# Keys' high rope rows, low rope rows and high nope rows in one 128-row tile; low nope keys as one 64-row product per head

## The reference, cut to what matters

```python
q = (rmsnorm(cq, q_norm_g) @ w_uq).reshape(bsz, S, B_HEADS, B_NOPE + B_ROPE)   # 16 heads, 64 + 32
qn, qr = q[..., :B_NOPE], apply_rope(q[..., B_NOPE:], cos, sin)
...
s = (jnp.einsum('bqhd,bkhd->bhqk', qn_b, kn_all)            # 768 keys: 256 of the context, 512 tokens
     + jnp.einsum('bqhr,bkr->bhqk', qr_b, kr_all)).astype(jnp.float32) * scale
p = jax.nn.softmax(s, axis=-1).astype(dt)
return jnp.einsum('bhqk,bkhd->bqhd', p, v_all)
```

## Time and profile before

| what | value |
|---|---|
| median of 3 runs | 1159.51 us (1159.49 to 1160.32) |
| the profiled execution | 1159.5 us |
| its span on the core | 1157.7 us |
| granted TensorE clock, mean | 0.997 of full speed |
| PE busy | 1099.8 us, 95% of the span |
| DVE busy | 734.3 us, 63% |
| ACT busy | 649.0 us, 56% |
| POOL busy | 419.3 us, 36% |
| layer B's attention | from 562.8 us to some 735 us of the span |

### The profile page before, as it was taken

How to read it: one execution, slowest core, us unless ns; L and a number is a source line. 1 busy time by engine, 2 the same in 40 slices (tenths; PEclk the granted TensorE clock), 3 DMA queues, 4 the chain that set the end, 5 groups by cost and what they waited for, 6 DMA issues and landing times.

```text
span 1157.7 us, 20235 instructions
## 1 busy us (share of the span) xinstructions
PE 1099.8 (95%) x7430; PEld 900.7 (78%) x7430; DVE 734.3 (63%) x1590; ACT 649.0 (56%) x1355; POOL 419.3 (36%) x513
## 2 busy tenths in 40 slices
PE   5999999999998899999899999999999999999996
PEld 2678778877885689877688887898878777888785
DVE  7575766676568625363787787745767775527745
ACT  5604555555556526643677777846567753457733
POOL 2633012212120334675400002416654326456781
PEclk9999999999999999999999999999999999999998
DMA  9741424322114521130201101053212403213112
GB/s 373 253 163 46 176 107 162 133 108 101 46 29 173 204 81 37 40 109 35 57 14 34 65 10 47 1 166 87 73 46 78 151 19 128 91 56 121 44 37 73
DMA packets 34253, 109.33 MB, mean 94 GB/s; under 512 B 4516, under 2 KB 7076, under 8 KB 33772
## 3 DMA queue, kind: packets, MB, share of 16 engines
q1 hardware_dynamic: 34156, 108.05, 27.7%
HBM read 101.39 MB, written 2.11 MB: 89 GB/s over the span
## 4 chain that ended last, share of the span: by engine, by line
PE 75%; DVE 12%; ACT 5%; issue 3%; POOL 2%; DMA 2%; SPq 1%; DVEq 0%; POOLq 0%; ACTq 0%
PE PS L677 31%; PE PS L660 15%; PE PS L794 8%; PE PS L782 7%; PE PS L983 6%; PE PS L1051 3%; DMA AF<-wstream 2%; PE PS L712 2%; DVE AD L2372 1%; ACT AF L1272 1%; DVE AF L2069 1%; POOL AR L2553 1%; DVE AR L2273 1%; PE PS L884 1%; PE PS L693 1%
## 5 line engine op out<-in xcount | busy, mean ns | idle before, releaser
L2553 POOL TENSOR_TENSOR AR<-AF,AR 128x256 fp32r<-128x256 f32 x396 | 304.5, 802 | 585.2 <-ACT AR L1152 585.2
L677 PE MATMUL PS<-AR 128*128 128x512 f32 (+1 forms) x2208 | 450.5, 360 | 4.7 <-POOL AR L2553 1.4
L677 PEld LDWEIGHTS PS<-AR 128*128 128x128 f32 x2208 | 364.0, 189 | 72.6 <-issue 10.5
L660 PE MATMUL PS<-AR 128*128 128x256 f32 (+4 forms) x1284 | 244.9, 327 | 6.7 <-ACT AF L1272 1.7
L660 PEld LDWEIGHTS PS<-AR 128*128 128x128 f32 (+1 forms) x1284 | 179.8, 190 | 41.7 <-issue 20.6
L1281 ACT ACTIVATE AF<-PS 128x512 f32<-128x512 f32 (+3 forms) x192 | 124.6, 649 | 100.0 <-PE PS L782 96.0
L1272 ACT ACTIVATE AF<-PS,AF 128x512 f32<-128x512 f32 (+3 forms) x192 | 140.8, 733 | 27.2 <-DVE AF L2349 18.3
L782 PE MATMUL PS<-AF 128*128 128x128 f32 x864 | 127.4, 274 | 8.4 <-DVE AF L1990 5.9
L782 PEld LDWEIGHTS PS<-AF 128*128 128x128 f32 x864 | 100.1, 140 | 32.9 <-issue 15.5
L1152 ACT ACTIVATE AR<-AF 128x1024 fp32r<-128x1024 f32 x99 | 103.3, 1052 | 35.3 <-PE PS L983 27.9
L794 PE MATMUL PS<-AF 128*64 128x128 f32 x1728 | 115.3, 278 | 3.4 <-DVE AF L1997 2.5
(11 more groups left out here) (216 smaller groups left out, 1147.2 us busy)
## 6 DMA issues: line engine op xcount, KB each, us to landing
AF<-wstream SPq DMA_DIRECT2D x171, 512.0 KB, 5.0
AF<-x_in SPq DMA_DIRECT2D x2, 1024.0 KB, 8.5
AD<-rows SPq DMA_DIRECT2D x4, 512.0 KB, 5.9
out<-AF SPq DMA_DIRECT2D x16, 128.0 KB, 1.9
AF<-AF SPq DMA_DIRECT2D x28, 64.0 KB, 2.0
AF<-rpb_band SPq DMA_DIRECT2D x8, 224.0 KB, 5.2
BIAS<-rpb_band SPq DMA_DIRECT2D x8, 224.0 KB, 4.7
AF<-ctx_in SPq DMA_DIRECT2D x1, 1024.0 KB, 5.5
```

The costliest lines, as they stand in the source:

```text
L660: mm = pe.matmul(out, stationary, moving, start=i == 0, stop=i == len(products) - 1)
L677: mm = pe.matmul(out[:, 0:t1 - t0], a, b, start=k == 0 and i == 0, stop=k == nk - 1 and i == 2)
L2553: ins = pool.tensor_tensor(w[:, 1, at:at + 256], raw(c)[:, at:at + 256], w[:, 0, at:at + 256].bitcast(F32), ALU.subtract)
```

## The change

The keys of a head now lie in one tile of 128 rows (`KB`): high nope (64), high rope (32) and low rope (32); for the second half the nope rows stand in rows 64 to 127 and the rope rows in 0 to 63. The low nope keys have a buffer of their own (`KBL`), the first half in rows 0 to 63, the second in rows 64 to 127. The queries have their rope rows twice. So a unit has two products of 128 rows for each stretch of keys where it had three of 96 rows, plus one of 64 rows, high nope query by low nope key.

The 64-row products of both halves of a step are issued together, in a new function `scores_low(m)` ahead of `scores(2m)`. It opens the sums of both score buffers, so it waits for the exponentials of both units of the step before.

The order changes with it. On PE the filler stands ahead of `weigh_values`. On ACT both exponentials of a step stand ahead of `turned(2m-1)`. SP issues 8 DMAs for the rope queries of a pair where it had 4, and 7 for the rope keys where it had 3.

```diff
-                    pairs = ((0, 0), (0, 1), (1, 0))
-                    q = [QB[0:96, a, p % 2, half, t * P:t * P + P] for a in range(2)]
-                    k = [KB[0:96, b, p % 2, half, :] for b in range(2)]
+                    q = [QB[:, a, p % 2, half, t * P:t * P + P] for a in range(2)]
+                    k, k_low = KB[:, p % 2, half, :], KBL[ROWS_OF[half], p % 2, :]
                     unit(c0=256, c1=1024, segments=[
-                        (256, C, [(q[a], k[b][:, S:T]) for a, b in pairs]),
-                        (512, S, [(q[a], k[b][:, 0:S]) for a, b in pairs])],
+                        (256, C, [(q[a], k[:, S:T]) for a in range(2)]),
+                        (512, S, [(q[a], k[:, 0:S]) for a in range(2)])],
+                         low=[(512, S, q[0][ROWS_OF[half]], k_low[:, 0:S]), (256, C, q[0][ROWS_OF[half]], k_low[:, S:T])],
...
+            def scores_low(m):
+
+                pe.wait_ge(exp_done, 2 * m)
+                for a, b in zip(units[2 * m]["low"], units[2 * m + 1]["low"]):
+                    for n, (c0, width, stationary, moving) in ((2 * m, a), (2 * m + 1, b)):
+                        pe.matmul(score_bank(n)[:, c0:c0 + width], stationary, moving, start=True, stop=False)
...
+                        if "low" in units[2 * m]:
+                            banks_read(m == m0, 2, 3)
+                            scores_low(m)
                         scores(2 * m)
...
+                    low = "low" in units[2 * m0]
+                    if low and (m < m1 or values_first):
+                        for name in fillers(m):
+                            make(name)
                     if not ahead and m0 <= m - behind - 1 < m1:
                         weigh_values(m - behind - 1)
-                    if m < m1 or values_first:
+                    if not low and (m < m1 or values_first):
                         for name in fillers(m):
                             make(name)
...
-                pe.wait_ge(qb_in[p % 2], 64 * (p // 2 + 1))
+                pe.wait_ge(qb_in[p % 2], 128 * (p // 2 + 1))
...
                     if m < m1:
                         exps(2 * m)
+                    if m < m1 and is_b(2 * m):
+                        exps(2 * m + 1)
                     if m > m0:
                         turned(2 * m - 1)
-                    if m < m1:
+                    if m < m1 and not is_b(2 * m):
                         exps(2 * m + 1)
...
-                sp.dma_start(KB[64:96, :, buf, half, :].bitcast(F32), KB[64:96, :, 0, 0, :].bitcast(F32)).then_inc(kr_in[buf], 16)
+                r = TURNED_ROWS[half]
+                if buf or half:
+                    sp.dma_start(KB[r:r + 32, buf, half, :].bitcast(F32), KB[64:96, 0, 0, :].bitcast(F32)).then_inc(kr_in[buf], 16)
+                sp.dma_start(KB[r + 32:r + 64, buf, half, :].bitcast(F32), KRL.bitcast(F32)).then_inc(kr_in[buf], 16)
...
-                        sp.dma_start(QB[64:96, a, p % 2, half, :].bitcast(F32),
-                                     src[rows, h // 4, :].bitcast(F32)).then_inc(qb_in[p % 2], 16)
+                        for r in (TURNED_ROWS[half], TURNED_ROWS[half] + 32):
+                            sp.dma_start(QB[r:r + 32, a, p % 2, half, :].bitcast(F32),
+                                         src[rows, h // 4, :].bitcast(F32)).then_inc(qb_in[p % 2], 16)
```

More of the change, by code:

```diff
@@ L391, in build @@
         SQX = [PPT[:, i * S:i * S + S] for i in range(3)] + [PPT[:, 3 * T + i * S:3 * T + i * S + S] for i in range(4)]
-        KB = tiles(R1, 2, 2, 2, T)
+        KB, KBL, KRL = tiles(R1, 2, 2, T), tiles(R1[:, 4 * T:], 2, T), R1[64:96, 6 * T:7 * T]
+        TURNED_ROWS = [64, 0]
         QB = tiles(R1[:, 6144:], 2, 2, 2, S)
@@ L592, in is_c, with is_b @@
             return n >= 2 * B_END
+        def is_b(n):
+            return 2 * A_END <= n < 2 * B_END
         def score_bank(n):
@@ L656, in chunk_ready, with sum_of @@
                 pe.wait_ge(lo_done, split_at[name] + 1)
-            def sum_of(out, products):
+            def sum_of(out, products, begun=False):
                 for i, (stationary, moving) in enumerate(products):
-                    mm = pe.matmul(out, stationary, moving, start=i == 0, stop=i == len(products) - 1)
+                    mm = pe.matmul(out, stationary, moving, start=i == 0 and not begun, stop=i == len(products) - 1)
                 return mm
@@ L772, in scores @@
                 for c0, width, products in u["segments"]:
-                    mm = sum_of(score_bank(n)[:, c0:c0 + width], products)
+                    mm = sum_of(score_bank(n)[:, c0:c0 + width], products, begun="low" in u)
                 mm.then_inc(s_ready, 1)
+            def scores_low(m):
[3 more added lines that the diff above has]
+                        pe.matmul(score_bank(n)[:, c0:c0 + width], stationary, moving, start=True, stop=False)
             def turn(n):
@@ L950, in ready_b @@
                 pe.wait_ge(b_ready, p + 1)
-                pe.wait_ge(qb_in[p % 2], 64 * (p // 2 + 1))
+                pe.wait_ge(qb_in[p % 2], 128 * (p // 2 + 1))
                 if p < 2:
-                    pe.wait_ge(kr_in[p], 16 * (p + 1))
+                    pe.wait_ge(kr_in[p], (48, 64)[p])
             attend(A_END, B_END, ready_b,
@@ L1436, in evac_b @@
                 for half in range(2):
-                    dst = QB[0:64, 0, p % 2, half, :] if name[2] == "q" else KB[0:64, 0, p % 2, half, t0:t1]
+                    dst = QB[ROWS_OF[half], 0, p % 2, half, :] if name[2] == "q" else KB[ROWS_OF[half], p % 2, half, t0:t1]
                     ins = act.activation(dst, acc[64 * half:64 * half + 64, 0:t1 - t0], ACT.Copy)
@@ L2164, in low_b @@
                 for half in range(2):
-                    buf = QB[0:64, :, p % 2, half, :] if name[2] == "q" else KB[0:64, :, p % 2, half, t0:t1]
-                    ins = dve.tensor_tensor(buf[:, 1, :], acc[64 * half:64 * half + 64, 0:t1 - t0],
-                                            buf[:, 0, :].bitcast(F32), ALU.subtract)
+                    rows = ROWS_OF[half]
+                    high, low = ((QB[rows, 0, p % 2, half, :], QB[rows, 1, p % 2, half, :]) if name[2] == "q" else
+                                 (KB[rows, p % 2, half, t0:t1], KBL[rows, p % 2, t0:t1]))
+                    ins = dve.tensor_tensor(low, acc[rows, 0:t1 - t0], high.bitcast(F32), ALU.subtract)
                 read(ins, name)
@@ L2619, in _ @@
             pool.wait_ge(lo_done, fed[0])
-            pool.tensor_copy(KB[64:96, 0, 0, 0, :], KRF[64:96, :]).then_inc(kr_high, 1)
+            pool.tensor_copy(KB[64:96, 0, 0, :], KRF[64:96, :]).then_inc(kr_high, 1)
             pool.wait_ge(kr_high, 1)
-            pool.tensor_tensor(KB[64:96, 1, 0, 0, :], KRF[64:96, :], KB[64:96, 0, 0, 0, :].bitcast(F32),
-                               ALU.subtract).then_inc(kr_split, 1)
+            pool.tensor_tensor(KRL, KRF[64:96, :], KB[64:96, 0, 0, :].bitcast(F32), ALU.subtract).then_inc(kr_split, 1)
             pool.wait_ge(kr_split, 1)
@@ L2767, in others @@
                     sp.wait_ge(kr_split, 1)
+                    load_roped_keys(0, 0)
                     load_roped_keys(0, 1)
```

## The result

The changed kernel takes 1179.02 us (median of 4 runs, 1176.92 to 1180.59), the kernel before 1159.88 beside it (4 runs, 1159.49 to 1160.32): ratio 1.0162 with a 95% interval of 1.0149 to 1.0175. That is 19.1 us more, where 17.6 were predicted. The profiled execution is the one of 1180.59 us (its span is 1178.8).

A forecast was written before the change was run, and what follows sets the result against it. PE was taken to bound the kernel, with DVE only 4.6 us short of it per pair. Seven pairs 14.4, last pair 0.8 and start 2.4 made 17.6 us on 1159.5: 1177.1 us, range 1166 to 1190.

The forecast's parts named there:

- The products: On PE, a step's four 64-row products take 0.35 us with halves side by side; serial rival 0.70, chance 0.15.
- the border: On PE, changing between half-size and full-size work costs 0.1 us on either side; bounds per step 0 and 0.4.
- Scores under the copy: Second unit's scores shorten by 0.35 us, worth 0, because 1.81 us between a step's two transposes stay.
- PE's own path: PE's work per step without the ring: 6.78, 6.09, 5.75 and 5.39 us, 24.0 a pair instead of 23.28.
- the sum's 0.8: Last pair, which has no fillers: steps go from 5.21 to 5.39 us, 0.8 us in sum.
- The ring: Loop from exponential through PE, DVE and ACT to the next exponential: 4.95, 6.37, 6.37 and 5.82 us; not binding: 0.13.
- Step 3: Last of a pair's steps 0 to 3: 4.95 plus 0.87 us for DVE's low part of the filler, 5.82.
- that sign: PE would idle ahead of the 64-row products in steps 2, 3 and 0, released by ACT's exponential.
- The seventh pair: Pair where ACT splits weights: counted at 2.06 us more like other pairs with fillers; the split adds nothing.
- The start: Attention's beginning: extra DMAs in SP's queue put first scores at 566.0 and first transposes at 572.2, costing 2.4 us.
- The granted clock: PE's idling of some 3 us at the start may lower its clock: 0 to 2 us, not in the sum.
- The filler's wait: In step 1 the filler waits some 0.1 to 0.3 us for bank 7, freed by DVE's low part; not added.

The follow-up runs named there:

- the low part out of the way: Changed kernel with DVE writing only 16 columns of each low part of a filler for pairs 1 to 7: 1169.18 us, ratio 1.0078.
- full-height products: Changed kernel with four 128-row products per step in place of the 64-row ones: 1183.55 us, ratio 1.0202.
- The joint wait alone: Kernel before, with layer B's scores(2m) also waiting for both exponentials of the step before, products and order unchanged: 1171.02 us, ratio 1.0098.
- by halves: Changed kernel with the four 64-row products reordered, both of the first half, then both of the second: 1180.03 us, ratio 1.0168.

## Why the prediction was right, step by step

**The products: right.** Two start together, four in 0.35 plus the border (0.55 to the scores), and the same rows would have cost 11.2 us more.

**Scores under the copy are worth nothing: right.** 1.81 us stayed, and a third less of the second unit alone moved nothing (0.9996).

**PE's own path: right to 0.05.** 6.11, 5.74, 5.44 and 6.79 with the low part out of the way, against 6.09, 5.75, 5.39 and 6.78. In the last pair a step takes 5.40 instead of 5.21; the sum's 0.8 for it was rounded up, since 5.39 - 5.21 four times is 0.7. The 0.1 on either side of a border carries this; the full-height products, slower by 4.5 us instead of 11, show it from the other side.

**The ring: right, step 3 short.** Predicted 6.37, 6.37 and 5.82, measured 6.44, 6.35 and 5.95 (the first of them held by a second path as well). The joint wait alone costs 11.9 us in the kernel before, and the low part 9.8 in the changed one. Step 3 was mis-sized by 0.13, and the row was there: 0.87 stood for the low part of a 256-column filler, but the trace of before has 1.00 from its start to the second maximum, as the changed kernel has (639.58 to 640.58).

```profile
628.56 0.85 DVE L2166 TENSOR_TENSOR AR<-PS,AR 64x256 fp32r<-64x256 f32 x2
...
629.56 0.96 DVE L2007 TENSOR_REDUCE AF<-PS 128x1 f32<-128x768 f32 x1
```

PE's idle time ahead of the 64-row products was said to be released by ACT's exponential, in steps 2, 3 and 0. Over 575 to 750 us PE shows it eight times, once in the first pair and then at the start of step 0 of each pair; its weight loads show it 14 times. At the start of step 2 of a steady pair (630.60) PE has no idle time, so that sign was not met: step 1 had waited for bank 7 instead (who waits <- for whom: us in total, times, longest us):

```profile
PEld PS L785 <- ACT AF L1290: 5.2, 14, 1.7
PE PS L785 <- ACT AF L1290: 4.4, 8, 1.2
PEld PS L681 <- DVE AR L2188: 4.2, 13, 0.4
```

**The seventh pair: too much.** 2.06 was counted for it as for the others. It takes 25.5 like them, but before it took 24.4 already, stretched by ACT's split of weights. The ring swallows that stretch, so this pair cost 1.1. "Adds nothing" was right, but the sum should have been made against this pair's own length. The other six cost 2.23 each where 2.06 stood. Up to the last step's first scores the trace has 6 x 2.23 + 1.1 + 0.6 = 15.1, which is 20.0 - 5.0, and the sum had 15.2 for all steps. That these two errors cancel is luck.

**The start: the size right, the cause in part wrong.** With the query DMAs in place the first scores were said to start at 566.0, and start at 567.25 less the 1.37 of this execution, 565.9. The 2.4 us are there at full clock too (14.45 against 12.07, by halves). But they were put down to SP's queue, and without the four extra query DMAs 1.6 of them stay: the loads were only the last of the waits by 0.8 us, and DVE's copy of the second unit's banks, which the joint opening waits for in the first step, was in no term. The granted clock adds 1.2 in the changed kernel's profiled execution and nothing there by halves. It had been named with 0 to 2 us and left out of the sum. With 1.2 the sum is 18.8, against 19.1; how much of it the median holds is not shown.

**The end of the attention** was in no term. The last values but one come 2.79 us after those ahead of them instead of 2.27; with ACT's old order it is 2.26. So the new order of the exponentials costs 0.5 there.

**The filler's wait** for bank 7 was put at 0.1 to 0.3 and not added. It is 0.30 in step 1 and has no slack there: with it PE's path ends at 630.60, and the ring ends no later. It would be worth 0.06 to 0.15 in that step if it went alone (an estimate from the two lags above).

**What was wrong in the experiments' reasons:** that PE starts products strictly in order, that ACT's order is worth something in steps 0 and 3, that the joint wait gives the old kernel steps of 6.4, and that the loads alone hold up the start.

**Open:** what the order of fillers alone is worth in the changed kernel, what the 1.6 us of the start consist of, and why steps 0 and 3 save less than 0.35 when the first unit's third is gone.

## What to carry to other kernels

When work from two units is merged into one group, the group takes on the latest of both units' waits. Before counting its columns, follow the released buffer once round through every engine and add up the loop; in the kernel before, one wait cost 12 us where the columns saved promised 11. In this kernel, columns taken away between the first transposes and the copy that the second ones wait for were worth nothing, and the same columns ahead of it 6.5 us: find the copy first. And look for a second path that ends together with the one that you found; here both hung on one row of DVE.

## What the runs showed of the hardware

- Products on rows 0 to 63 and 64 to 127 start 2 to 7 ns apart (two of 512 columns, then two of 256 columns 0.34 us later); on the same rows the four start at 0, 0.335, 0.564 and 0.681 us. A product on free rows starts ahead of one written before it that waits for its rows, in all 32 steps.
- A change of shape costs 0.1 us on either side of the border: 0.55 us to the scores for 0.35 of 64-row products, and then 0.82 to the transposes instead of 0.70. The Trainium skill ("TensorEngine Tiling (Array Packing)", key properties) names the drain; a half-height group saves 0.35 us of products and gives 0.2 of it back.
- After 3.02 us in which PE waited for DMAs the granted clock was 0.50 (1.2 GHz) from 566.2 to 572.9, and 512-column products started 0.43 apart instead of 0.23. After 3.03 us of the same wait in the run by halves it was 1.00 over the first products and 0.50 from 576.7 to 580.0. Without the extra DMAs, with 2.24 us of waiting, it stayed at 1.00. So the same wait cost the first transposes 1.2 us in one execution and nothing in another.
